# Moving a hybrid block's per-head steps to other places among its weight pieces

## The reference, cut to what matters

```python
# x (1, 256, 2048) float32; one layer
h = rms_norm(x, norm1_g)
proj = h @ w_in                      # 2048 x 7168: retention q, k, v, gate; attention q, k, v
ret = head_group_norm(retention(rotary(rq), rotary(rk), rv), ret_norm_g)   # 8 heads of 128
ret = silu(rg) * ret
att = chunk_attention(rms_norm(aq, q_norm_g), rms_norm(ak, k_norm_g), av, rel_bias)  # 8 heads
x = x + concat([ret, att]) @ w_out   # 2048 x 2048
h = rms_norm(x, norm2_g)
x = x + square(relu(h @ w_ff1)) @ w_ff2     # 2048 x 8192, 8192 x 2048
```

## Time and profile before

| | |
|---|---|
| median of 3 runs | 1125.01 us (1124.82 to 1125.35) |
| the profiled execution, its own time | 1125.35 us |
| its span in the trace | 1123.6 us |
| TensorE busy | 1104.4 us, 98% of the span |
| VectorE busy | 884.8 us, 79% |
| ScalarE busy | 688.9 us, 61% |
| mean granted TensorE clock | 0.997 |
| transfers | 263.81 MB, 235 GB/s on average |

### The profile page before, as it was taken

How to read it: one execution, slowest core, us unless ns; L and a number is a source line. 1 busy time by engine, 2 the same in 40 slices (tenths; PEclk the granted TensorE clock), 3 DMA queues, 4 the chain that set the end, 5 groups by cost and what they waited for, 6 DMA issues and landing times.

```text
span 1123.6 us, 13185 instructions
## 1 busy us (share of the span) xinstructions
PE 1104.4 (98%) x5198; PEld 933.6 (83%) x5198; DVE 884.8 (79%) x881; ACT 688.9 (61%) x809; POOL 54.2 (5%) x66
## 2 busy tenths in 40 slices
PE   9799999999999999999999999999999999999998
PEld 9688988988888888888888888888888888888887
DVE  6877777787787768878788778788779788779784
ACT  6665564575565446667756577755667755577652
POOL 0100100100100000000000000000000000000000
PEclk9899999999999999999999999999999999999999
DMA  9874585584576556696797797797787797787782
GB/s 356 266 244 168 160 268 174 168 261 162 176 249 262 187 216 196 225 291 214 244 277 247 239 284 225 228 295 229 259 262 232 242 278 234 258 275 222 247 276 95
DMA packets 42958, 263.81 MB, mean 235 GB/s; under 512 B 4752, under 2 KB 6544, under 8 KB 15120
## 3 DMA queue, kind: packets, MB, share of 16 engines
q1 hardware_dynamic: 36992, 221.00, 52.5%
q0 software_dynamic: 5760, 41.95, 20.2%
q10 hardware_dynamic: 144, 0.02, 0.0%
HBM read 260.85 MB, written 2.10 MB: 234 GB/s over the span
## 4 chain that ended last, share of the span: by engine, by line
PE 85%; DVE 7%; ACT 3%; issue 2%; POOL 1%; ACTq 0%; DVEq 0%
PE acc L866 10%; PE acc L870 10%; PE acc L868 10%; PE acc L738 5%; PE acc L745 5%; PE acc L751 5%; PE bankC L828 4%; PE acc L828 4%; PE bankC L821 4%; PE acc L821 4%; PE acc L823 4%; PE bankC L823 4%; DVE w_lo L1399 3%; PE acc L590 2%; PE acc L595 2%
## 5 line engine op out<-in xcount | busy, mean ns | idle before, releaser
L1686 DVE TENSOR_TENSOR w_lo<-raw,w_hi 128x2048 fp32r<-128x2048 f32 x180 | 410.9, 2289 | 126.8 <-ACT w_hi L1202 126.6
L1202 ACT ACTIVATE w_hi<-raw 128x2048 fp32r<-128x2048 f32 x180 | 344.7, 1916 | 219.9 <-PE acc L870 144.9
L1399 DVE TENSOR_TENSOR w_lo<-raw,w_hi 128x1024 fp32r<-128x1024 f32 (+1 forms) x152 | 167.5, 1106 | 54.5 <-ACT w_hi L992 54.4
L992 ACT ACTIVATE w_hi<-raw 128x1024 fp32r<-128x1024 f32 (+1 forms) x152 | 143.2, 964 | 42.2 <-DVE raw L1408 32.4
L738 PE MATMUL acc<-w_hi,hT_hi 128*128 128x384 f32 (+1 forms) x416 | 105.6, 372 | 0.3 <-ACT w_hi L992 0.3
L866 PE MATMUL acc<-w_hi,hF_hi 128*128 128x512 f32 x256 | 100.8, 394 | 0.0
L870 PE MATMUL acc<-w_hi,hF_lo 128*128 128x512 f32 x256 | 99.7, 390 | 0.0
L868 PE MATMUL acc<-w_lo,hF_hi 128*128 128x512 f32 x256 | 99.6, 389 | 0.0
L745 PE MATMUL acc<-w_hi,hT_lo 128*128 128x384 f32 (+1 forms) x416 | 99.3, 357 | 0.0
L751 PE MATMUL acc<-w_lo,hT_hi 128*128 128x384 f32 (+1 forms) x416 | 98.9, 356 | 0.0
L866 PE MATMUL acc<-w_hi,dF_hi 128*128 128x512 f32 x248 | 96.8, 390 | 0.0
(11 more groups left out here) (262 smaller groups left out, 1813.6 us busy)
## 6 DMA issues: line engine op xcount, KB each, us to landing
raw<-in_w_up SPq DMA_DIRECT2D x64, 1024.0 KB, 5.9
raw<-in_w_down SPq DMA_DIRECT2D x64, 1024.0 KB, 5.8
raw<-in_w_ret SPq DMA_DIRECT2D x32, 1024.0 KB, 5.0
raw<-in_w_att SPq DMA_DIRECT2D x28, 768.0 KB, 4.2
raw<-in_w_out SPq DMA_DIRECT2D x16, 1024.0 KB, 4.9
raw<-in_w_up POOLq DMA_DIRECT2D x16, 1024.0 KB, 8.9
raw<-in_w_down POOLq DMA_DIRECT2D x16, 1024.0 KB, 8.8
raw<-in_w_ret POOLq DMA_DIRECT2D x8, 1024.0 KB, 8.5
```

The source lines that it names most:

```text
L992: nc.scalar.activation(piece(w_hi, q, 0, n), raw[:, r, half * n:(half + 1) * n], ACT.Copy).then_inc(hi_done, 1)
L1202: nc.scalar.activation(w_hi[:, ring(s)], raw[:, r, :], ACT.Copy).then_inc(slab_hi, 1)
L1399: nc.vector.tensor_tensor(piece(w_lo, q, 0, n), raw[:, IN_PLAN[i, READ_AT.get(step, step)][0], half * n:(half + 1) * n], piece(w_hi, q, 0, ...
L1686: nc.vector.tensor_tensor(w_lo[:, ring(s)], raw[:, r, :], w_hi[:, ring(s)].bitcast(f32), ALU.subtract).then_inc(slab_lo, 1)
```

## The change

Three things are moved, with no arithmetic added or taken away.

1. At the start, the two halves of the first weight slab are no longer issued by SyncE but by ScalarE, the first one ahead of the gains, the second one behind them.
2. The steps of the heads stand at other places, most of them one piece earlier: on TensorE `att_T` at 12 and 26 (13 and 27 before), `att_scores` at 14 and 27 (15, 28), `att_PT` at 18 and 30 (19, 31), `att_pv` at 20 and 32 (21, 33), `ret_T`, `ret_scores`, `ret_y` of the even retention head at 34, 35, 36 (35, 36, 37), its `ret_ZT` behind piece 0 of the next block (1). ScalarE and VectorE have the steps in between moved to match. On ScalarE `att_squares` of the second head changes places with `set_y`. On VectorE `set_w` comes one piece later, and the first `in_sum` of a block comes one piece earlier and now stands ahead of `att_norm`.
3. In block 0, `s_first` stands behind the conversion of piece 10 rather than of piece 9, `s_third` at 9 rather than 12, and `s_hi` and `s_lo` up to two pieces earlier.

```diff
             for q in range(PIECES):                                   # SyncE
+                if s > 0:
+                    sp.dma_start(raw[:, s, o * half_w:(o + 1) * half_w], ...
...
+            half_w = PIECE_KT * N_ATT                                 # ScalarE
+            nc.scalar.dma_start(raw[:, 0, 0:half_w], w_att[0:P, 0:half_w]).then_inc(half_in[0], 16)
             nc.scalar.dma_start(gv[:], gains).then_inc(gains_in, 16)
+            nc.scalar.dma_start(raw[:, 0, half_w:2 * half_w], w_att[0:P, half_w:2 * half_w]).then_inc(slab_in[0], 16)
...
-                at_piece(i, 35, ret_T, 2 * i)                         # TensorE
+                at_piece(i, 34, ret_T, 2 * i)
...
-            at_piece(0, PIECES - 1, s_first)                          # VectorE
+            at_piece(0, 8, s_first)
             at_piece(0, 8, s_second)
+            at_piece(0, 9, s_third)
...
                 at_piece(i, 10, att_mean_squares, h)
+                at_piece(i, 10, in_sum, i, "b", "Q1")
                 at_piece(i, 11, att_norm, h)
-                at_piece(i, 11, in_sum, i, "b", "Q1")
```

More of the change, by code:

```diff
@@ L457, in _ @@
                              x_pieces[:, q * half_x:(q + 1) * half_x]).then_inc(xc_in[q], 16)
[L458 to L460 removed]
+                if s > 0:
+                    sp.dma_start(raw[:, s, o * half_w:(o + 1) * half_w],
+                                 w_att[s * P:(s + 1) * P, o * half_w:(o + 1) * half_w]).then_inc(
+                                     slab_in[s] if o else half_in[s], 16)
             x_rows = x.rearrange("b (m p) d -> p (b m) d", p=P)
@@ L769, in _ @@
             for i in range(BLOCKS):
-                for h, places in ((2 * i, (13, 15, 19, 21)), (2 * i + 1, (27, 28, 31, 33))):
-                    for pos, f in zip(places, (att_T, att_scores, att_PT, att_pv)):
-                        at_piece(i, pos, f, h)
-                at_piece(i, 35, ret_T, 2 * i)
-                at_piece(i, 36, ret_scores, 2 * i)
-                at_piece(i, 37, ret_y, 2 * i)
-                at_piece(i + 1, 1, ret_ZT, 2 * i)
+                for h, first in ((2 * i, 12), (2 * i + 1, 26)):
+                    at_piece(i, first, att_T, h)
+                    at_piece(i, (14, 27)[h % 2], att_scores, h)
+                    at_piece(i, (18, 30)[h % 2], att_PT, h)
+                    at_piece(i, (20, 32)[h % 2], att_pv, h)
+                at_piece(i, 34, ret_T, 2 * i)
+                at_piece(i, 35, ret_scores, 2 * i)
+                at_piece(i, 36, ret_y, 2 * i)
+                at_piece(i + 1, 0, ret_ZT, 2 * i)
                 late = i == BLOCKS - 1
@@ L1135, in _ @@
             at_piece(0, PIECES - 1, x_squares)
-            for f, pos in enumerate((9, 10, 13, 14)):
+            for f, pos in enumerate((9, 10, 12, 13)):
                 at_piece(0, pos, s_hi, f)
@@ L1142, in _ @@
                 at_piece(i, 12, keep_in_q1, i)
-                at_piece(i, 13, att_qT, h)
+                at_piece(i, 12, att_qT, h)
                 at_piece(i, 16, keep_in_p5, i)
-                at_piece(i, 17, att_exp, h)
-                at_piece(i, 19, att_pT, h)
-                at_piece(i, 21, att_mix, h)
+                at_piece(i, 16, att_exp, h)
+                at_piece(i, 18, att_pT, h)
+                at_piece(i, 20, att_mix, h)
                 at_piece(i, 22, att_proj, h + 1)
-                at_piece(i, 23, set_y, i)
-                at_piece(i, 24, att_squares, h + 1)
+                at_piece(i, 23, att_squares, h + 1)
+                at_piece(i, 24, set_y, i)
                 at_piece(i, 25, set_h, i)
-                at_piece(i, 27, att_qT, h + 1)
-                at_piece(i, 29, att_exp, h + 1)
-                at_piece(i, 31, att_pT, h + 1)
+                at_piece(i, 26, att_qT, h + 1)
+                at_piece(i, 28, att_exp, h + 1)
+                at_piece(i, 30, att_pT, h + 1)
                 at_piece(i, 32, ret_proj, u)
[L1156 to L1159, removed]
+                at_piece(i, 32, att_mix, h + 1)
+                at_piece(i, 33, ret_exp, u)
+                at_piece(i, 34, ret_qT, u)
+                at_piece(i, 37, ret_scale, u)
                 at_piece(i + 1, 0, ret_proj, u + 1)
-                at_piece(i + 1, 1, ret_mix, u)
+                at_piece(i + 1, 0, ret_mix, u)
                 at_piece(i + 1, 0 if late else 2, ret_exp, u + 1)
@@ L1618, in _ @@
             at_piece(0, PIECES - 1, x_mean_squares)
-            at_piece(0, PIECES - 1, s_first)
+            at_piece(0, 8, s_first)
             at_piece(0, 8, s_second)
+            at_piece(0, 9, s_third)
             at_piece(0, 10, s_lo, 0)
[L1622 to L1625, removed]
+            at_piece(0, 11, s_lo, 1)
+            at_piece(0, 13, s_lo, 2)
+            at_piece(0, 15, s_lo, 3)
             for i in range(BLOCKS):
@@ L1628, in _ @@
                 at_piece(i, 10, att_mean_squares, h)
+                at_piece(i, 10, in_sum, i, "b", "Q1")
                 at_piece(i, 11, att_norm, h)
-                at_piece(i, 11, in_sum, i, "b", "Q1")
-                at_piece(i, 13, att_kT, h)
+                at_piece(i, 12, att_kT, h)
                 at_piece(i, 14, in_sum, i, "d", "P5")
-                at_piece(i, 15, att_bias_max, h)
-                at_piece(i, 18, att_probs, h)
+                at_piece(i, 14, att_bias_max, h)
+                at_piece(i, 17, att_probs, h)
                 at_piece(i, 20, set_z, i)
-                at_piece(i, 21, att_mix, h)
-                at_piece(i, 23, set_w, i)
+                at_piece(i, 20, att_mix, h)
+                at_piece(i, 24, set_w, i)
                 at_piece(i, 24, att_mean_squares, h + 1)
[L1639 to L1642, removed]
+                at_piece(i, 25, att_norm, h + 1)
+                at_piece(i, 26, att_kT, h + 1)
+                at_piece(i, 27, att_bias_max, h + 1)
+                at_piece(i, 29, att_probs, h + 1)
+                at_piece(i, 32, att_mix, h + 1)
                 at_piece(i, 33, ret_rotate, u)
-                at_piece(i, 33, att_mix, h + 1)
                 at_piece(i, 34, ret_rotated, u)
-                at_piece(i, 35, ret_kT, u)
+                at_piece(i, 34, ret_kT, u)
                 at_piece(i, 35, ret_sigmoid, u)
-                at_piece(i, 36, ret_decay, u)
-                at_piece(i, 37, ret_norm, u)
+                at_piece(i, 35, ret_decay, u)
+                at_piece(i, 36, ret_norm, u)
                 at_piece(i + 1, 0 if late else 1, ret_rotate, u + 1)
                 at_piece(i + 1, 0 if late else 2, ret_rotated, u + 1)
-                at_piece(i + 1, 1, ret_mix, u)
+                at_piece(i + 1, 0, ret_mix, u)
                 at_piece(i + 1, 1 if late else 3, ret_kT, u + 1)
```

## The result

| | before | after |
|---|---|---|
| median, us | 1124.91 (1124.41 to 1125.35) | 1133.37 (1133.17 to 1133.98, 4 runs) |
| ratio | | 1.0077, 95% interval 1.0058 to 1.0094 |
| profiled execution / span, us | 1125.35 / 1123.6 | 1134.24 / 1132.4 |
| mean granted clock | 0.997 | 0.995 |

The change costs 8.5 us. I had forecast 1125.6, no change, with 1131.0 as the upper end: the prediction was wrong. It had put 0.30 on a slower kernel, and even its slowest rival, A in full, stood at 1132.5.

The account below looks back on a forecast made before the run. TensorE, 98% busy, was taken as the bound, its waits a chain over VectorE and ScalarE. Block terms +1.3 - 0.2 - 0.2 - 0.5 = +0.4 us gave 1125.6 us, range 1121.0 to 1131.0.

Parts of the forecast that it names:

- A: Rival, slower: the clock falls at the new 1.7 us `ret_T` wait in four blocks, +6.8, 1132.5 us; chance 0.15.
- What bounds the kernel: TensorE, busy 98% of the span; only its waits, some 19 us, or lost clock can move; none after 400 us.
- The sum: Blocks 0 to 3 together: +1.3 - 0.2 - 0.2 - 0.5 = +0.4 us, forecast 1125.6 us, no change.
- A steady block, first half: Pieces 12 to 20: new `a_qk` wait of 1.2 us, old waits gone or smaller; gain 1.3 us.
- Second half: Piece 20 to piece 4 of the next block: new `ret_T` wait of 1.7 us; loses 1.1 us.
- Block 0: TensorE waits 2.5 us inside piece 11, over 4 at `att_T`; block loses 1.3 us, bounds -1 and +5.5.
- the two clock falls of before: Block 0, over 32 to 36 and 40 to 48 us: clock falls behind waits, each costing 1.7 us.
- The transfers: At the start: gains land 0.4 to perhaps 1.5 us later, hidden; `Q1` transfers start 0 to 0.9 sooner, taken as 0.4.
- B: Rival, slower: longer waits (`a_qk` 2, `ret_T` 2.3), start block loses 3; +5.7, 1131 us; chance 0.15.
- C: Rival, faster: ScalarE and VectorE run ahead, `ret_T` wait 1.0, first-half gain 1.5; -3.5, 1121.5 us; chance 0.23.
- D: Rival: earlier-placed steps still start when their input allows, every wait only renamed; 1125 us; chance 0.47 together with the forecast.

Follow-up runs that it names:

- b_insum: The kernel before with only the first `in_sum` of a block moved ahead of `att_norm` on VectorE; 1115.70 us, ratio 0.9919.
- b_even: The kernel before with the even attention head's steps one piece earlier and `in_sum` ahead of `att_norm`; 1120.62 us, ratio 0.9965.
- e_ms_early: The kernel after with one more step moved: the odd head's `att_mean_squares` at piece 23, ahead of `set_w`; 1131.48 us, ratio 1.0059.
- b_odd: The kernel before with only the odd attention head's steps moved, `att_squares` ahead of `set_y` and `set_w` a piece later; 1135.26 us, ratio 1.0092.
- b_odd_swap: The kernel before with the odd attention head's steps moved, but `set_y` ahead of `att_squares` and `set_w` where they were; 1129.29 us, ratio 1.0041.
- b_ret: The kernel before with only the even retention head's steps and what feeds them one piece earlier; 1134.65 us, ratio 1.0088.
- e_odd_back: The kernel after with the odd attention head's steps back at their old places, retention steps still early; 1136.67 us, ratio 1.0110.
- e_s_back: The kernel after with `s_first`, `s_third`, `s_hi` and `s_lo` of block 0 back at their old places; 1130.39 us, ratio 1.0053.

## Why the prediction was wrong, point by point

**What bounds the kernel** held: only waits moved, and the part behind 400 us is as long as before.

**The sum** was +1.3 for block 0, -0.2 for each of blocks 1 and 2, and -0.5 for block 3. Measured by the timelines they are +3.8, +1.8, +1.8 and +1.5. The waits that I looked for were mostly there and of my size; the terms that I set too low are block 0 behind its `att_T` and the second half of every block, block 3 among them, where I expected a gain and showed no walk.

**A steady block, first half.** Forecast: gain 1.3; measured 0.8. The new wait for `a_qk` was walked rightly (1.2, measured 1.18). In the timeline `att_T` and `att_PT` start 1.35 and 0.25 us later than the piece ahead of them allows, 1.6 where I put 1.3, and the pieces are 0.2 longer than I took them. A larger mistake is in what I did with the number. I summed `in_sum`'s gain and the early `att_T`'s wait into one number and took both as the price of one move. They are two edits: `in_sum` alone is worth 2.2 us a block, and the early `att_T` takes 1.4 of it away for nothing (`b_insum`, `b_even`).

**Second half.** Forecast: loses 1.1; measured 2.6. `ret_T`'s wait was right (1.7, with bounds of 1.5 and 1.9; measured 1.79), and so was the end of the odd head's `r_qk` wait. Wrong is "`att_T`, scores and `att_PT` of the second head find their inputs within 0.1 us": `att_T` waits 0.41, and I gave `set_w` 0.2 without what stopping and starting adds. The terms that I named for this half, 0.2 + 0.1 + 1.7 - 0.6, also add up to 1.4 and not to 1.1. In the timeline TensorE's next row starts later than in an undisturbed run of the same rows by 0.6 at that `att_T`, 0.4 at `set_w`, and 1.95 at `ret_T`, where the rows name 0.41, 0.21 and 1.79: each stop costs about 0.2 more than the wait that is named. `att_PT` starts 0.2 late too, and the end of the odd head's `r_qk` wait gives 0.75 back where 0.58 was named. Together 0.4 + 0.6 + 0.2 + 1.95 - 0.75 = 2.4 of the 2.6 us. The 0.41 itself is GpSimd's power, which took 1.03 before and takes 1.93 here; `e_ms_early` takes that away and 1.9 of 8.5 us with it.

**Block 0.** Forecast +1.3; measured +3.8. The waits came as walked: 3.2 inside piece 11 where I said 2.5, and `att_T` at 43.53 where I said 43.9 less 0.4 for the transfers. What failed is the stretch behind it: piece 20 starts 15.8 us behind `att_T`, and I had allowed 14.4 to 15.1, so it is 1.2 late instead of 0.2. I showed no walk of the softmax there. `a_p` is done at 56.81, and at 56.85 in `e_ms_early`, which is the same kernel up to there, though its scores start 0.9 sooner; so `att_PT` could hardly come before 56.8. It comes at 57.58. That last 0.7 goes with the low clock, 0.50 until 48.5 us: in `e_ms_early`, where the clock is back at 1.00 by 47, `att_PT` starts at 56.91.

I also expected the two clock falls of before to be worth 1.7 us each. They were worth nothing. `b_odd`, `b_odd_swap` and `b_ret` are the same as before up to piece 25. Over 40 to 44 and 44 to 48 us the clock is at 0.84 and 0.74 in the kernel before, at 1.00 and 1.00 in `b_odd`, 0.78 and 0.79 in `b_odd_swap`, 0.96 and 0.62 in `b_ret`, and yet `att_PT` comes 27.4 us behind the first `Q1` matmul in all four (57.8 - 30.4, 57.3 - 29.9): TensorE at half its clock only waited less, above all for `a_p`. The times agree: of the kernel before, 11 executions with a mean clock of 1.000 have a median of 1125.0 us, and 23 with 0.998 one of 1124.7.

The second half of block 0 lost 2.6 like that of any other block, where I had put 1.1. The `s_` steps, undone, give 3.0 back.

**The transfers** were hidden, as said. The gains landed at 6.03 instead of 4.53 us, the worse end of my range (5.86 to 6.15 in the eight traces with the new start, 4.24 to 4.63 in those with the old); this agrees with the rule of queue order that the prediction cites. The first `Q1` weights came 1.3 us sooner in this pair of traces and 0.9 on average, where I took 0.4.

**The rivals.** A (the clock falls at `ret_T`) is false for this kernel, at 1.8 us; at 2.3 it came true in `b_ret` and `e_odd_back`. B (longer waits, 1131) was nearest in kind, but for another reason: not longer `a_qk` and `ret_T`, but the odd head, GpSimd and block 0. The full A comes nearest in time (1132.5), with no fall behind any `ret_T`: that is chance. C's gain was there, 9.1 us in one step, and the rest of the change spent it twice. D (every wait only renamed), which shared the forecast's 0.47, is false: most new waits cost more than the old ones that they replace.

## What to carry to other kernels

Price each moved step by itself, and test it by itself: a move that only puts a consumer ahead of its producer can gain nothing, and hides the gain of the one that puts a producer earlier. On an engine that is 98% busy, move a step of the bounding engine earlier only where the trace shows its input lying ready, and count some 0.2 us for each stop above the wait that the trace names. Before a low clock is counted as a loss, ask whether the engine had its inputs: in block 0 of the kernel before it had not, and the falls cost nothing; behind `ret_T` in `b_ret` it had, and a fall cost 1.4 us.

## What the runs showed of the hardware

GpSimd's small power (128x4) took 1.03, 1.65, 1.93, 2.98 or 4.46 us, by what VectorE ran beside it. In the kernel after it ends 0.88 us behind the end of `sf_lo` (42.57 against 41.69), and 0.89 behind that of the conversion at 158.59 (160.70 against 159.81); in `e_ms_early`, with VectorE idle at its start, it took 1.03. The 2.98 of block 1 ends 0.87 behind `in_sum` (132.94 against 132.07), though the conversion of 131.98 to 132.93 runs beside it; so not every operation of VectorE holds it, and which do stays open. The growth of these powers is the 10 us that GpSimd's busy time grew. The Trainium skill, SBUF — State Buffer, section "SBUF: two separate sides", has a rule for this: a VectorE operation with two SBUF inputs and a GpSimd operation that reads SBUF lock each other out for a whole instruction, whichever starts first. The traces agree as far as GpSimd's waits behind `in_sum`, `sf_lo` and the conversion at 158.59 go, and not in the case just named; that VectorE is held in turn they don't show, since the conversion at 155.53 in `e_ms_early`, which starts while the power runs, took 1.22 us as anywhere else.

```profile
155.53 1.22 DVE L1408 TENSOR_TENSOR w_lo<-raw,w_hi 128x1024 fp32r<-128x1024 f32 x1 [0.78 <-ACT w_hi L998]
```

The length of a single wait does not decide the clock here: in block 0 it fell behind one of 2.2 us in the kernel before and not behind one of 3.3 in `e_s_back`; in later blocks not behind 1.8, and behind some of 2.3. What decides stays open.
